# Forgetting attention: two of four probability tiles scaled by VectorE, the widest transposes read out by ScalarE

## The reference, cut to what matters

```python
def forgetting_attention(q, k, v, f_logit, f_bias):
    ...
    qf = q.astype(jnp.float32) * (HEAD_DIM ** -0.5)
    ...
    log_f = jax.nn.log_sigmoid(f_logit.astype(jnp.float32) + f_bias.astype(jnp.float32))
    c = jnp.cumsum(log_f, axis=1).transpose(0, 2, 1)

    def blk(i):
        ...
        mask = pos[None, :] <= tq[:, None]
        s = jnp.einsum('bqhd,bshd->bhqs', qb, kf) + cq[..., None] - c[:, :, None, :]
        p = jax.nn.softmax(jnp.where(mask, s, -jnp.inf), axis=-1)
        return jnp.einsum('bhqs,bshd->bqhd', p, vf)
```

## Time and profile before

| | us |
|---|---|
| median of 3 runs | 2368.73 |
| lowest and highest | 2367.63, 2368.8 |
| the profiled execution, its own time | 2362.22 |
| its span (first to last instruction) | 2360.5 |
| first start of the product with the values (pair 0) | at 1058.75 |
| the same product of pair 7 | at 1130.73 |
| transposes and scaling of all pairs | 1046.6 to 1130 |

### The profile page before, as it was taken

How to read it: one execution, slowest core, us unless ns; L and a number is a source line. 1 busy time by engine, 2 the same in 40 slices (tenths; PEclk the granted TensorE clock), 3 DMA queues, 4 the chain that set the end, 5 groups by cost and what they waited for, 6 DMA issues and landing times.

```text
span 2360.5 us, 25614 instructions
## 1 busy us (share of the span) xinstructions
PE 2119.1 (90%) x9416; PEld 1626.8 (69%) x9416; DVE 1167.5 (49%) x2097; ACT 731.9 (31%) x1228; POOL 440.5 (19%) x338
## 2 busy tenths in 40 slices
PE   8977999789999978998889999959999687999996
PEld 6766667668788766875678887845445536888875
DVE  4332345576346343237566256262406654867744
ACT  3210345323223213245243123122213205443441
POOL 2100000000000000039100000000020004767774
PEclk9985789789999998999989999979999897999998
DMA  5231100135335312210235235211110002233333
GB/s 203 90 116 45 27 19 19 54 127 184 116 106 197 107 54 107 96 49 2 108 126 194 89 134 203 109 56 37 72 71 36 18 36 90 107 121 111 125 127 122
DMA packets 39828, 224.91 MB, mean 95 GB/s; under 512 B 5920, under 2 KB 6368, under 8 KB 20144
## 3 DMA queue, kind: packets, MB, share of 16 engines
q1 hardware_dynamic: 27840, 181.17, 21.3%
q0 software_dynamic: 11888, 42.39, 5.7%
HBM read 215.61 MB, written 2.10 MB: 92 GB/s over the span
## 4 chain that ended last, share of the span: by engine, by line
PE 80%; DVE 10%; POOL 5%; ACT 3%; issue 1%; DMA 1%; SPq 0%; POOLq 0%; DVEq 0%; ACTq 0%
PE G L401 33%; PE G L1934 7%; PE TR L1934 4%; PE OB L1934 4%; PE G L905 3%; PE G L1857 3%; PE G L1661 3%; PE OB L1682 2%; POOL SC_sb L682 2%; PE G L1876 2%; PE OB L1004 1%; PE G L1832 1%; DVE stat_sb L2381 1%; PE G L1995 1%; PE G L907 1%
## 5 line engine op out<-in xcount | busy, mean ns | idle before, releaser
L401 PE MATMUL G<-xt_high,weights_high 128*128 128x512 f32 x1128 | 450.0, 399 | 21.1 <-DVE weights_low L424 16.1
L401 PE MATMUL G<-xt_low,weights_high 128*128 128x512 f32 x1128 | 444.0, 394 | 0.0
L401 PE MATMUL G<-xt_high,weights_low 128*128 128x512 f32 x1128 | 443.5, 393 | 0.0
L424 DVE TENSOR_TENSOR weights_low<-ring_sb,weights_high 128x1024 fp32r<-128x1024 f32 x196 | 234.9, 1206 | 385.4 <-ACT weights_high L418 385.3
L418 ACT ACTIVATE weights_high<-ring_sb 128x1024 fp32r<-128x1024 f32 x284 | 293.8, 1044 | 373.8 <-PE OB L1934 136.9
L401 PEld LDWEIGHTS G<-xt_high,weights_high 128*128 128x128 f32 x1128 | 213.8, 190 | 71.4 <-issue 23.4
L401 PEld LDWEIGHTS G<-xt_low,weights_high 128*128 128x128 f32 x1128 | 213.8, 190 | 47.5 <-issue 3.5
L401 PEld LDWEIGHTS G<-xt_high,weights_low 128*128 128x128 f32 x1128 | 213.6, 189 | 46.7 <-issue 1.4
L424 POOL TENSOR_TENSOR weights_low<-ring_sb,weights_high 128x1024 fp32r<-128x1024 f32 x88 | 213.1, 2437 | 74.0 <-ACT weights_high L418 74.0
L1426 DVE SCALAR_TENSOR_TENSOR KS_sb<-G,cols_sb,KS_sb 128x441 f32<-128x441 f32 (+2 forms) x176 | 120.8, 686 | 75.1 <-ACT KS_sb L1182 75.1
L1599 POOL DMA_DIRECT2D KS_sb<-ada x64 | 33.8, 529 | 572.6 <-DVE og_sb L2280 572.6
(11 more groups left out here) (432 smaller groups left out, 3677.4 us busy)
## 6 DMA issues: line engine op xcount, KB each, us to landing
ring_sb<-chunks SPq DMA_DIRECT2D x142, 1024.0 KB, 4.8
KS_sb<-ada POOLq DMA_DIRECT2D x64, 512.0 KB, 4.7
ring_sb<-slabs SPq DMA_DIRECT2D x10, 2048.0 KB, 7.8
qb_sb<-wide_sb SPq DMA_DIRECT2D x24, 128.0 KB, 2.2
X_sb<-x SPq DMA_DIRECT2D x4, 512.0 KB, 6.6
rows_sb<-ln_gain POOLq DMA_DIRECT2D x4, 512.0 KB, 5.3
rows_sb<-ln_bias POOLq DMA_DIRECT2D x4, 512.0 KB, 6.0
out<-X_sb SPq DMA_DIRECT2D x4, 512.0 KB, 4.9
```

Of the source, the lines that this page charges most:

```text
L401: mm = nc.tensor.matmul(out, lhsT=a, rhs=b, start=(3 * i + j == 0), stop=(3 * i + j == n - 1))
L424: tt_(out=Wl[:, n % 4, c], in0=raw_quarter(Q)[:, c], in1=Wh[:, n % 4, c], op=ALU.subtract).then_inc(w_lo, 1)
```

## The change

GpSimd keeps the scaling of blocks 0 and 1 and loses that of blocks 2 and 3, which VectorE takes, in its list behind `copy(n, 0)` and `copy(n, 1)`. VectorE loses `copy(n, 4)` and `copy(n, 5)`, which ScalarE takes at the end of its iteration, behind `exp(n+1, 3)`. The semaphores for "scaled" and "read out" are split in two, and the waits of `turn` and `attended` follow. Nothing else moves.

```diff
+        SCALED_POOL = 2
...
+        def turned_pair(k):
+
+            t, es = TURNS[k]
+            ps = TR[k % 2][:, 0:len(es) * (t + 1) * P].rearrange("p (u b c) -> p u b c", u=len(es), b=t + 1)
+            return PTU[:, es[0]:es[-1] + 1, 0:t + 1, t * P:(t + 1) * P], ps
...
             def turn(n, k):
                 t, es = TURNS[k]
-                pe.wait_ge(pair_scaled, 8 * n + 2 * t + es[-1] + 1)
-                if 6 * n + k >= 2:
-                    pe.wait_ge(pair_copied, 6 * n + k - 1)
+                if t < SCALED_POOL:
+                    pe.wait_ge(pair_scaled, 2 * SCALED_POOL * n + 2 * t + es[-1] + 1)
+                else:
+                    pe.wait_ge(pair_scaled_dve, 2 * (TT - SCALED_POOL) * n + 2 * (t - SCALED_POOL) + es[-1] + 1)
+                if k >= 2:
+                    pe.wait_ge(pair_copied, 4 * n + k - 1)
+                elif n:
+                    pe.wait_ge(pair_copied_act, 2 * n + k - 1)
...
             def attended(n):
...
-                pe.wait_ge(pair_copied, 6 * n + 6)
+                pe.wait_ge(pair_copied, 4 * n + 4)
+                pe.wait_ge(pair_copied_act, 2 * n + 2)
...
+            def copy(n, k):
+                act.wait_ge(pair_turned, 6 * n + k + 1)
+                dst, ps = turned_pair(k)
+                nc.scalar.activation(dst, ps, ACT.Copy).then_inc(pair_copied_act, 1)
...
                 exp(n + 1, 2)
                 exp(n + 1, 3)
+                copy(n, 4)
+                copy(n, 5)
...
+            def scale(n, t):
+                dve.wait_ge(pair_rec, 4 * n + t + 1)
+                for e in range(2):
+                    p = pair_scores(n, e, t)
+                    nc.vector.tensor_scalar(p, p, rsp[:, n % 2, t, e:e + 1], None, ALU.mult).then_inc(pair_scaled_dve, 1)
...
                 copy(n, 0)
+                scale(n, 2)
                 copy(n, 1)
+                scale(n, 3)
                 mixed_low(n - 1)
...
                 invert(n + 1, 1)
-                copy(n, 4)
-                copy(n, 5)
...
             for n in range(N_FOX):
-                scale(n, 2)
-                scale(n, 3)
                 stage_low(n + 2)
                 scale(n + 1, 0)
                 scale(n + 1, 1)
```

More of the change, by code:

```diff
@@ L362, in build @@
         pair_turned = sem("pair_probabilities_transposed")
-        pair_copied = sem("pair_transposes_copied")
+        pair_scaled_dve = sem("pair_probabilities_scaled_by_vector")
+        pair_copied = sem("pair_transposes_copied_by_vector")
+        pair_copied_act = sem("pair_transposes_copied_by_scalar")
         pair_out = sem("pair_attended_in_psum")
@@ L629, in copy @@
             def copy(n, k):
-                t, es = TURNS[k]
                 dve.wait_ge(pair_turned, 6 * n + k + 1)
-                ps = TR[k % 2][:, 0:len(es) * (t + 1) * P].rearrange("p (u b c) -> p u b c", u=len(es), b=t + 1)
-                nc.vector.tensor_copy(PTU[:, es[0]:es[-1] + 1, 0:t + 1, t * P:(t + 1) * P], ps).then_inc(pair_copied, 1)
+                dst, ps = turned_pair(k)
+                nc.vector.tensor_copy(dst, ps).then_inc(pair_copied, 1)
+            def scale(n, t):
[3 more added lines that the diff above has]
+                    nc.vector.tensor_scalar(p, p, rsp[:, n % 2, t, e:e + 1], None, ALU.mult).then_inc(pair_scaled_dve, 1)
             def mixed_low(n):
```

## The result

| | before | after |
|---|---|---|
| median of 5 runs each, us | 2367.63 | 2379.04 |
| lowest and highest | 2365.94, 2368.8 | 2377.23, 2382.0 |
| ratio, 95% interval | | 1.005 (1.0039 to 1.006) |
| the profiled execution, its own time | 2362.22 | 2377.23 |

The change costs 11.4 us, 0.5%. GpSimd's busy time falls by 42 us (440.5 to 398.1), and the kernel is slower. The two profiled executions are 15.0 us apart, not 11.4; where the difference lies is worked out in the part on why the prediction was right.

What follows compares the result with a forecast made beforehand. GpSimd was taken to bound the stage, and a ring of waits through the other engines afterwards. Gaps +8.5, hand-over +0.4 and clock +1.6 gave +10.5 on 2368.73: 2379 us, own range 2375 to 2383, wider range 2370 to 2388.

Steps and rivals of the forecast that it cites:

- GpSimd is the bound before: Stage of the change: GpSimd, busy 10.00 of 10.00 us, sets the pace at 10.95 us a pair.
- The ring of 11.16 us: Closed round of waits through TensorE, VectorE and ScalarE after the change, without slack: 11.16 us a pair against 10.95.
- The scalings' cost: VectorE's new scalings of blocks 2 and 3: 0.66 and 0.80 us, 1.46 a pair in its list.
- The contest for the port: VectorE's scalings wait for GpSimd's splits on a shared path: 1.06 us a round, making 12.22.
- the second wait (0.65): VectorE's scale(n, 3) waits 0.65 us for GpSimd's second split, after scale(n, 2) waited 0.4 for the first.
- the worse contest: Rival: a split between block 2's scalings, waits 0.4 + 1.24, 0.6 more in five rounds; 2382 to 2388; chance 0.14.
- The sum of the gaps at the full clock: Starts of pair 0's to pair 7's product: 5 x 12.22 + 11.16 + 8.20 = 80.5 us against 71.98, +8.5.
- The clock: TensorE products slowed at 1.2 GHz now count in the round: two or three hit, 0.7 net each, +1.6 us.
- The hand-over: End of the stage: VectorE's two low parts start 1.1 us later, with mixed_low(7) behind them, +0.4 us.
- Pair 0's product: First iteration: its start was left where it was, with an error of 1 us either way allowed.

Runs made afterwards that it cites:

- e1: Changed kernel, but all scaling stays on GpSimd, so only the two read-outs move to ScalarE; 2366.34 us, ratio 1.0004 to the kernel before.
- e3: Changed kernel, but GpSimd's two splits of pairs 2 to 7 treat 32 columns instead of 512; 2366.71 us, ratio 1.001 to the kernel before.
- e8: Changed kernel, with each GpSimd split of pairs 2 to 7 made twice, once into an unread tile; 2384.08 us, ratio 1.008 to the kernel before.
- e9: Changed kernel executed a second time, unaltered, for its profile alone; 2377.25 us in one execution.
- e2: Changed kernel, but VectorE keeps all read-outs, so only the scalings move; 2373.92 us, ratio 1.0037 to the kernel before.
- e4: Changed kernel, but VectorE scales blocks 2 and 3 before the first read-out of a round; 2358.16 us, ratio 0.9974 to the kernel before.
- e6: As e5, but ScalarE makes its two wide read-outs ahead of the last two exponentials; 2343.96 us, ratio 0.9913 to the kernel before.
- e5: As e4, but VectorE's low part of the result moved to the end of its iteration; 2353.95 us, ratio 0.996 to the kernel before.
- e7: As e2, but VectorE scales blocks 2 and 3 before the first read-out; 2354.71 us, ratio 0.9958 to the kernel before.

## Why the prediction was right, step by step

- **GpSimd is the bound before.** Right: its relief by 42 us of busy time moved the bound; e1 leaves it there and nothing changes.
- **The ring of 11.16 us.** Right: 11.02 in e3, e8 and e9, wherever a round had no wide split and no slow product (and 10.32 for the 10.45 of e2). e4 and e6 show it from the other side, since taking terms off it took the time off.
- **The scalings' cost,** 0.66 and 0.80 from the earlier trace rows. Right: where free, they are 0.41 and 0.47 long, and from the first of a block to VectorE's next instruction it is 0.65 and 0.79 (1139.98 to 1140.63, 1141.23 to 1142.02).
- **The contest for the port,** 1.06 a round. Right that GpSimd's splits hold the scalings up, and a little small: 12.25 - 11.02 = 1.23. The working of it was wrong in part. It had the second wait (0.65) at `scale(n, 3)`; that one meets none in any of the rounds. What came out is the order that the prediction named as the worse contest, a split between the two scalings of block 2, at 0.17 + 1.02 instead of that rival's 0.4 + 1.24: the first split starts 2.20 us behind the product (1060.66 to 1062.86) and not 2.43 - 0.05 = 2.38, so less of it is left when the first scaling comes. That the sum of the waits came near is in part luck; in e2, where the split starts 2.66 behind the product, this order costs 1.64.
- **The sum of the gaps at the full clock,** 80.5. Right as far as it can be put together: 5 x 12.25 + 11.02 + 8.2 = 80.5. The last gap was never measured at the full clock; its 8.2 is the prediction's own. In e3 it is 9.96 behind a product that took 1.66 more than at the full clock, which leaves 8.3.
- **The clock,** 1.6 us. The mis-sized term. In the gaps, 85.33 and 84.22 less 80.5 are 4.8 and 3.7 us. Behind them the last product, slow both times, adds 1.7 and 2.2 more (from its start to the projection 5.54 and 5.95 us, 3.80 before): 6.5 and 5.9 in all. I had two or three slow products at 0.7 net each. In the middle rounds they cost less, 12.49 to 12.58 against 12.25, some 0.3: pair 2's product is 1.3 us longer, but the scalings behind it come when the splits are almost over and wait 0.17 instead of 1.19. What was missed is the end: behind the last splits no wait for GpSimd absorbs a slow product, so it counts in full, 1.4 to 2.2 each, and slow transposes come on top (1.94 for 1.09 us).
- **The hand-over,** 0.4. Not seen: VectorE's two low parts ended at 1149.23, ahead of the slow last product, whose own low part started at 1150.79.
- **Pair 0's product** starts 17.54 us behind the first scores (at 1043.12) where it was 16.74 (from 1042.01), 0.8 later, inside the 1 us set aside.

**The total.** The forecast of 2379 met a median of 2379.04, and that is closer than its terms were. It started from a median of three runs 1.1 above that of the five, and its +10.5 was worked out inside the profile. From the first scores to the first matmul of the projection the stage took 92.52 and 92.54 us in the two profiles of the kernel before, and 108.41 and 107.70 in those of the changed one, 15.9 and 15.2 more: 0.8 in front, 8.5 at the full clock and 6.5 or 5.9 by the clock. Behind the stage 1.9 and 1.2 us come back, for which no run shows a cause, so both pairs of profiles are 14.0 apart from the first scores to the end. The medians are 11.4 apart. The other 2.6 are most likely from ahead of the stage, though that isn't shown: nothing was changed there, and the two executions of the kernel before differ by 3.4 there (first scores at 1042.01 and 1045.42; at 1043.12 and 1043.08 in the changed one). So the mechanism and the 8.5 us of the full clock were right; that a clock term some 4 to 5 us too small left no trace in the median is luck.

The Trainium skill ("SBUF — State Buffer", section "Who interferes with whom") states that a two-port VectorE instruction and a GpSimd one exclude each other. e3 and e8 agree with it: the longest scaling takes 0.51 us beside short splits and 1.53 beside wide ones, and doubling the splits lengthens the round from 12.25 to 13.70.

## What to carry to other kernels

When work moves off the busiest engine, add up the round of waits that it moves into, instruction by instruction in the order of each list, before comparing busy shares: here the same relief of GpSimd lost 11 us or gained 20, according to the place of four scalings, two copies and one subtraction. Put work that is ready early into the stretch where its engine waits, and put read-outs that release the next step ahead of work that only the step after needs. And price an instruction for what runs beside it: a scaling of 0.41 us on VectorE took up to 1.43 us beside GpSimd's splits of some 1.3, while copies out of PSUM kept their time.

## What the hardware showed that was not expected

- VectorE's scalings and GpSimd's splits take turns instruction by instruction. Two scalings in direct succession were parted by a split (0.58 and then 1.43 us for a free duration of 0.41), and with each split made twice two of them took 2.68 us instead of 0.74. The order within the round decides the price: 1.23 us in the changed kernel, 1.64 in e2, for the same two splits and four scalings.
- A low busy share is no protection: at 3.89 us of work in 10, GpSimd still delayed VectorE by 1.23 us a round. In the kernel before it was never idle, and VectorE's copies out of PSUM took what they take now (681 ns for 512 columns, 0.68 us at 1065.63).
- The granted clock fell without any long pause: TensorE had idled no more than 1.27 us at a time in the round ahead of the first slow product (1072.91 to 1085.45). By their durations, two of eight products are slow in the kernel before, in e1 and in e2, four and three in the changed kernel, six in e8, one in e3 to e5, none in e6, where TensorE is busy 10.00 of 10 us, and none in e7, though TensorE idles there as in e4 (8.9 and 8.7 of 10). What in the pattern decides it the runs don't show.
